# Nine places in place of six for split weight chunks, three of them in memory that the stages share, and another order of VectorE's work at the seams between stages

## The reference

```python
x = x + 0.5 * swiglu(rmsnorm(x), ...)              # f1, hidden size 2816
h = rmsnorm(x); a_in, q, k, v, g = split(h @ w_in)
y_a = spatial_gating(gelu(a_in), ...)              # group norms of one half, mixed over rows
y_b = stick_breaking_attention(q, k, v)            # 16 heads
x = x + (g_a * (y_a @ w_branch_a) + g_b * (y_b @ w_branch_b)) @ w_out
x = rmsnorm(x + 0.5 * swiglu(rmsnorm(x), ...))     # f2
x = layer_norm(ALPHA * x + gla_mixer(x))           # gated linear attention, 4 heads
x = layer_norm(ALPHA * x + swiglu_ffn(x))          # f3
x = layer_norm(ALPHA * x + moba_mixer(x))          # rotary, causal attention, 8 heads
x = layer_norm(ALPHA * x + swiglu_ffn(x))          # f4
```

## Time and profile before

| | |
|---|---|
| runs (3) | 1272.39, 1273.16, 1273.42 us; median 1273.16 |
| profiled execution | 1272.88 us, its span 1271.1 us |
| granted TensorE clock | 0.999 of full |
| PE busy | 1253.1 us (99% of the span) |
| DVE, ACT busy | 759.4 us (60%), 604.3 us (48%) |
| mean DMA rate | 178 GB/s |

### The profile page before, as it was taken

How to read it: one execution, slowest core, us unless ns; L and a number is a source line. 1 busy time by engine, 2 the same in 40 slices (tenths; PEclk the granted TensorE clock), 3 DMA queues, 4 the chain that set the end, 5 groups by cost and what they waited for, 6 DMA issues and landing times.

```text
span 1271.1 us, 15302 instructions
## 1 busy us (share of the span) xinstructions
PE 1253.1 (99%) x5989; PEld 1023.2 (80%) x5989; DVE 759.4 (60%) x1023; ACT 604.3 (48%) x780; POOL 43.7 (3%) x99
## 2 busy tenths in 40 slices
PE   8999999999999999999999999999999999999999
PEld 6888887887777888888877657888887887888887
DVE  5755556756676665555456557555557767655554
ACT  6444435556657454444345434444434554444441
POOL 2000002100000000000000010000000000000000
PEclk9999999999999999999999999999999999999999
DMA  7756554755445466555555336655564544755551
GB/s 264 216 182 199 184 181 158 251 179 144 145 154 188 152 199 208 187 195 185 168 155 169 106 128 199 214 189 184 189 198 152 197 139 127 241 188 167 193 186 52
DMA packets 119767, 226.03 MB, mean 178 GB/s; under 512 B 8056, under 2 KB 16256, under 8 KB 119696
## 3 DMA queue, kind: packets, MB, share of 16 engines
q1 hardware_dynamic: 117120, 216.10, 52.1%
q0 software_dynamic: 2560, 8.95, 2.6%
q10 hardware_dynamic: 16, 0.00, 0.0%
HBM read 223.98 MB, written 1.05 MB: 177 GB/s over the span
## 4 chain that ended last, share of the span: by engine, by line
PE 92%; DVE 5%; issue 1%; POOL 1%; ACT 1%; DMA 0%; DVEq 0%; POOLq 0%; ACTq 0%
PE ps L409 28%; PE ps L412 28%; PE ps L417 28%; PE ps L370 3%; DVE wl L1444 2%; DVE X L1534 1%; DVE X L1540 1%; PE ps L738 1%; PE ps L740 1%; PE ps L569 1%; PE ps L582 1%; PE ps L874 0%; DVE XTL L1482 0%; DVE st L1525 0%; DVE X L1545 0%
## 5 line engine op out<-in xcount | busy, mean ns | idle before, releaser
L1444 DVE TENSOR_TENSOR wl<-raw,wh 128x1024 fp32r<-128x1024 f32 x409 | 487.4, 1219 | 247.1 <-ACT wh L903 244.5
L903 ACT ACTIVATE wh<-raw 128x1024 fp32r<-128x1024 f32 x409 | 422.8, 1055 | 227.3 <-PE ps L417 199.3
L409 PE MATMUL ps<-wh,XTH 128*128 128x512 f32 (+1 forms) x1184 | 453.4, 386 | 1.9 <-ACT wh L903 1.9
L412 PE MATMUL ps<-wl,XTH 128*128 128x512 f32 (+1 forms) x1184 | 445.5, 380 | 4.7 <-DVE wl L1444 4.7
L417 PE MATMUL ps<-wh,XTL 128*128 128x512 f32 (+1 forms) x1184 | 347.0, 379 | 0.2 <-DVE XTL L1482 0.2
L409 PEld LDWEIGHTS ps<-wh,XTH 128*128 128x128 f32 x1184 | 223.1, 188 | 47.7 <-issue 4.7
L412 PEld LDWEIGHTS ps<-wl,XTH 128*128 128x128 f32 x1184 | 223.3, 189 | 47.4 <-DVE wl L1444 7.9
L417 PEld LDWEIGHTS ps<-wh,XTL 128*128 128x128 f32 x1184 | 215.9, 188 | 43.6 <-DVE XTL L1482 1.3
L409 PE MATMUL ps<-wh,HHf 128*128 128x512 f32 x352 | 137.8, 391 | 0.0
L412 PE MATMUL ps<-wl,HHf 128*128 128x512 f32 x352 | 137.1, 390 | 0.0
L417 PE MATMUL ps<-wh,HLf 128*128 128x512 f32 x352 | 108.4, 389 | 0.0
(11 more groups left out here) (279 smaller groups left out, 941.6 us busy)
## 6 DMA issues: line engine op xcount, KB each, us to landing
raw<-in_ffn_w_gu_dram SPq DMA_DIRECT2D x88, 512.0 KB, 4.5
raw<-in_w_in_dram SPq DMA_DIRECT2D x56, 512.0 KB, 3.7
raw<-in_ff_w_gate_dram SPq DMA_DIRECT2D x44, 512.0 KB, 4.5
raw<-in_ff_w_up_dram SPq DMA_DIRECT2D x44, 512.0 KB, 4.8
raw<-in_ff_w_down_dram SPq DMA_DIRECT2D x44, 512.0 KB, 4.1
raw<-in_ffn_w_down_dram SPq DMA_DIRECT2D x44, 512.0 KB, 4.4
raw<-in_gla_w_in_dram SPq DMA_DIRECT2D x24, 512.0 KB, 4.5
raw<-in_moba_w_in_dram SPq DMA_DIRECT2D x24, 512.0 KB, 4.6
```

The costliest lines, as they stand in the source:

```text
L409: e.matmul(o, lh[:, kt, rows(t)], wh[:, s, w], start=kt == 0, stop=False)
L412: e.matmul(o, lh[:, kt, rows(t)], wl[:, s, w], start=False, stop=False)
L903: e.activation(wh[:, j % NS, 0:m], raw[:, j % NR, 0:m], ACT.Copy).then_inc(S("wh"), 1)
L1444: e.tensor_tensor(wl[:, j % NS, 0:m], raw[:, j % NR, 0:m], wh[:, j % NS, 0:m].bitcast(F32), ALU.subtract).then_inc(S("wl"), 1)
```

## The change

The number of places becomes nine. The six private ones stay; three more, wh2 and wl2 (24 KB a partition), are the first tiles of the memory in which each stage lays out its own. In the feed-forward stages and the MoBA stage a placeholder tile keeps that memory free. In the mixer it holds Q, K and V from block q0 on, until the first chunk of wb1 has been used, and in the GLA stage VV, KE, QDT, KIT and part of SS from gv0 until the first chunk of go0 has been used; during these stretches (`held`) only six places are given out. Each chunk takes the place that was used longest ago. `reach(n)` is the last chunk that can be split when chunk n has been used: with nine places `reach(j - 2)` is j + 7, with six it is j + 4.

For the opening blocks VectorE is held to the block's own chunks ahead of the readout of t = 0, and ScalarE to the block's end plus one; in the closing blocks VectorE makes one call between the two readouts. The 24 spare products are taken out.

```diff
+            wh2, wl2 = [sb(n, [P, MORE, 1024], FR, phase) for n in ("wh2", "wl2")]
...
+            sb("more_f2", [P, 2 * MORE, 1024], F32, phase)
...
-            QG, KG, LA = [sb(n, [P, 2, 512], F32, phase) for n in ("QG", "KG", "LA")]
-            VV, GG, O = [sb(n, [P, 2, D], F32, phase) for n in ("VV", "GG", "O")]
-            KE = sb("KE", [P, 2, 512], F32, phase)
+            VV = sb("VV", [P, 2, D], F32, phase)
+            KE = sb("KE", [P, 2, 512], F32, phase)
+            QDT, KIT = [sb(n, [P, 4, 256], F32, phase) for n in ("QDT", "KIT")]
+            SS = sb("SS", [P, 2, 3, 256], F32, phase)
...
+        held = [(first_chunk("q0"), first_chunk("wb1")), (first_chunk("gv0"), first_chunk("go0"))]
+        place, freed = [], []
+        last_use = [-NS - MORE + i for i in range(NS + MORE)]
+        for j in range(len(chunks)):
+            for begin, end in held:
+                if j == begin:
+                    last_use[NS:] = [end] * MORE
+            i = min(range(NS + MORE), key=lambda i: (last_use[i], i))
+            place.append(i)
+            freed.append(last_use[i])
+            last_use[i] = j
...
+        def reach(n):
+
+            j = max(n + 1, 0)
+            while j < len(chunks) and freed[j] <= n:
+                j += 1
+            return j - 1
+
+        OPENING, CLOSING = ("f1g0", "vg0", "f2g0", "gq", "f3g0", "mq0", "f4g0"), ("f1d1", "wo1", "f2d1", "go1", "f3d1",
+                                                                                  "mo1", "f4d1")
...
-            spare(4, left, wh[:, 0, 0:512], [six, seven])
...
```

In `act_program`:

```diff
-                    if j >= NS:
-                        e.wait_ge(S("used"), j - NS + 1)
+                    if freed[j] >= 0:
+                        e.wait_ge(S("used"), freed[j] + 1)
...
-                high_to(at_chunk["step"] + LEAD)
+                high_to(reach(at_chunk["step"] - 1))
...
-                    high_to(j - 1 + LEAD)
+                    high_to(reach(j - 2))
...
-                    high_to(end - tail - 1 + LEAD)
+                    ahead = reach(end - tail - 2)
+                    high_to(min(ahead, end + 1) if name in OPENING else ahead)
                     yield 0
                     for j in range(end - tail, end - 2):
-                        high_to(j + LEAD)
+                        high_to(reach(j - 1))
```

In `dve_program`:

```diff
-                low_to(at_chunk["step"] + LEAD)
+                low_to(reach(at_chunk["step"] - 1))
...
-                    low_to(j - 1 + LEAD)
+                    low_to(reach(j - 2))
...
-                    low_to(end - tail - 1 + LEAD)
+                    ahead = reach(end - tail - 2)
+                    low_to(min(ahead, end - 1) if name in OPENING else ahead)
                     yield 0
-                    for j in range(end - tail, end - 2):
-                        low_to(j + LEAD)
+                    for j in range(end - tail, end - tail + 1 if name in CLOSING else end - 2):
+                        low_to(reach(j - 1))
```

More of the change, by code:

```diff
@@ L18 @@
 NS = 6
-LEAD = NS - 1
+MORE = 3
 NEG = -1e30
@@ L120, in build @@
         with ExitStack() as phase:
+            VV = sb("VV", [P, 2, D], F32, phase)
+            KE = sb("KE", [P, 2, 512], F32, phase)
+            QDT, KIT = [sb(n, [P, 4, 256], F32, phase) for n in ("QDT", "KIT")]
+            SS = sb("SS", [P, 2, 3, 256], F32, phase)
+            STm = sb("STm", [P, 2, 2, 64], F32, phase)
+            GG, O = [sb(n, [P, 2, D], F32, phase) for n in ("GG", "O")]
             QG, KG, LA = [sb(n, [P, 2, 512], F32, phase) for n in ("QG", "KG", "LA")]
-            VV, GG, O = [sb(n, [P, 2, D], F32, phase) for n in ("VV", "GG", "O")]
-            KE = sb("KE", [P, 2, 512], F32, phase)
             E1 = sb("E1", [P, 2, 512], F32, phase)
-            QDT, KIT = [sb(n, [P, 4, 256], F32, phase) for n in ("QDT", "KIT")]
-            STm = sb("STm", [P, 2, 2, 64], F32, phase)
-            SS = sb("SS", [P, 2, 3, 256], F32, phase)
             lowT = sb("lowT", [16, 256], F32, phase)
@@ L197, in build, with first_chunk, wh_of, wl_of @@
         plan_ffn("f4", ffn_w_gu[1, :, 0:FF], ffn_w_gu[1, :, FF:], ffn_w_down[1])
+        def first_chunk(name):
+            return blocks[name][1]
+        held = [(first_chunk("q0"), first_chunk("wb1")), (first_chunk("gv0"), first_chunk("go0"))]
[9 more added lines that the diff above has]
+            last_use[i] = j
+        def wh_of(j):
+            return wh[:, place[j], :] if place[j] < NS else wh2[:, place[j] - NS, :]
+        def wl_of(j):
+            return wl[:, place[j], :] if place[j] < NS else wl2[:, place[j] - NS, :]
+        def reach(n):
[5 more added lines that the diff above has]
+                                                                                  "mo1", "f4d1")
         ev_count, mm0_count, seen = {}, {}, [0] * 4
@@ L398, in pe_products @@
             b, at, end, width, kts = blocks[name]
-            s, (_, n, _, k0) = j % NS, chunks[j]
+            _, n, _, k0 = chunks[j]
+            high, low = wh_of(j), wl_of(j)
             o = ps[:, bank_of(name, t), 0:width]
@@ L408, in pe_products @@
                     wait(e, "h", t, kt)
-                e.matmul(o, lh[:, kt, rows(t)], wh[:, s, w], start=kt == 0, stop=False)
+                e.matmul(o, lh[:, kt, rows(t)], high[:, w], start=kt == 0, stop=False)
                 if t == 0 and c == 0:
                     e.wait_ge(S("wl"), j + 1)
-                e.matmul(o, lh[:, kt, rows(t)], wl[:, s, w], start=False, stop=False)
+                e.matmul(o, lh[:, kt, rows(t)], low[:, w], start=False, stop=False)
             for c in range(n):
@@ L416, in pe_products @@
                     wait(e, "l", t, kt)
-                ins = e.matmul(o, ll[:, kt, rows(t)], wh[:, s, w], start=False, stop=kt == kts - 1)
+                ins = e.matmul(o, ll[:, kt, rows(t)], high[:, w], start=False, stop=kt == kts - 1)
             if t == 1:
@@ L649, in pe_gla @@
             b, at, end, width, kts = blocks["low"]
-            o, s = ps[0:16, bank_of("low", 0), 0:256], at % NS
+            o = ps[0:16, bank_of("low", 0), 0:256]
             e.wait_ge(S(f"ev{bank_of('low', 0)}"), ev_count["low", 0] - 1)
@@ L653, in pe_gla @@
             for kt in range(8):
-                hw, lw = [w[:, s, kt * 16:kt * 16 + 16] for w in (wh, wl)]
+                hw, lw = [w[:, kt * 16:kt * 16 + 16] for w in (wh_of(at), wl_of(at))]
                 e.matmul(o, hw, XTH[:, kt, :], start=kt == 0, stop=False)
@@ L899, in high_to @@
                     m = chunks[j][1] * chunks[j][2]
-                    if j >= NS:
-                        e.wait_ge(S("used"), j - NS + 1)
+                    if freed[j] >= 0:
+                        e.wait_ge(S("used"), freed[j] + 1)
                     e.wait_ge(S(f"raw{j % NR}"), 16 * (j // NR + 1))
-                    e.activation(wh[:, j % NS, 0:m], raw[:, j % NR, 0:m], ACT.Copy).then_inc(S("wh"), 1)
+                    e.activation(wh_of(j)[:, 0:m], raw[:, j % NR, 0:m], ACT.Copy).then_inc(S("wh"), 1)
                     at_chunk["next"] += 1
             def more():
-                high_to(at_chunk["step"] + LEAD)
+                high_to(reach(at_chunk["step"] - 1))
             def block(name, tail=0):
@@ L1214, in gla @@
                         copy_first("gq", QG, cols(0))
-                high_to(blocks["low"][1] - 1 + LEAD)
+                high_to(reach(blocks["low"][1] - 2))
                 def split_o(half):
@@ L1443, in low_to @@
                     e.wait_ge(S("wh"), j + 1)
-                    e.tensor_tensor(wl[:, j % NS, 0:m], raw[:, j % NR, 0:m], wh[:, j % NS, 0:m].bitcast(F32),
+                    e.tensor_tensor(wl_of(j)[:, 0:m], raw[:, j % NR, 0:m], wh_of(j)[:, 0:m].bitcast(F32),
                                     ALU.subtract).then_inc(S("wl"), 1)
@@ L1901, in gla @@
                         copy_second("gq", QG, cols(0))
-                low_to(blocks["low"][1] - 1 + LEAD)
+                low_to(reach(blocks["low"][1] - 2))
                 e.wait_ge(S("used"), blocks["low"][2])
```

11 lines of the change are left out of this document (7 added, 4 removed).

## The result

| | before | after |
|---|---|---|
| median of the runs | 1272.78 us (4 runs, 1272.31 to 1273.42) | 1281.55 us (4 runs, 1279.92 to 1283.25) |
| ratio | | 1.0065, 95% interval 1.0053 to 1.0077 |
| profiled execution; its span | 1272.88; 1271.1 us | 1283.25; 1281.5 us |
| granted TensorE clock | 0.999 | 0.993 |

The mean clock of after also counts the last 3.7 us of the kernel, which are at half clock and in which TensorE has nothing to do; in before the 24 spare products stand there.

What follows compares the result with a forecast made beforehand. TensorE, busy 1253.1 of 1271.1 us, was taken as the bound, so only its waits could be won. Gains of 7.4 and losses of 10.2 us gave +2.8 on 1272.88: 1275.7 us, range 1270 to 1279.3.

Steps and rivals of the forecast that it cites:

- Part 1: Stage openings: the last rows of a layer norm start earlier, a gain of 7.4 us together.
- Part 2: Places where three more splits come ahead of something TensorE needs: a loss of 10.2 us together.
- spare products: Kernel end: taking out the 24 products beside the last norm changes nothing, bounds 0 and 0.2 us.
- f1: Feed-forward f1 at the start: nine splits instead of seven make HB late, a loss of 1.9 us.
- wo0: wb1 and wo0: three more splits ahead of the merge delay YAL, a loss of 1.4 us, bounds 0.6 and 1.7.
- gk: GLA opening: QG's copy behind the split of gv0's late first chunk, a loss of 3.8 us, bounds 0 and 4.6.
- vg1: Mixer opening: first vg1 chunk split behind the group norm, 3.3 us lost, 1.4 us wait gone, net loss 1.9.
- MoBA key block: Between MoBA opening and key readout: rotary product late for the head transposes, 1.2 us loss, bounds 0 and 1.8.
- Rival 4: All upper bounds: U as late as now, wo0, GLA, MoBA at upper ends, late go0 load: 1279.2 us, chance 0.15.
- Rival 1: Parameter loads do not hold the weights up; losses of 3.8 and 1.2 us go: 1270.7 us, chance 0.17.
- rival 2: Catch-up hidden everywhere but in the mixer, readouts not behind the new splits: 1267.4 us, chance 0.1.
- rival 3: No effect: five raw buffers, not places, set the lead; seams and catch-ups both shrink: 1272.9 within 1, chance 0.08.

Runs made afterwards that it cites:

- settled version: Changed kernel with catch-ups held back at f1, wb1 to wo0 and gq to gk, and vg1's first chunks split before the group norm: 1263.98 us, ratio 0.9925.
- vg1 run: Changed kernel, but VectorE splits the first chunk of vg1 ahead of the group norms of vg0: 1278.40 us, ratio 1.0039 to before.
- GLA run: Changed kernel, but only six places are given out from gq to gk: 1274.94 us, ratio 1.0009 to before.

## Why the prediction was right or wrong

**Part 1 was right.** Every opening gained what was worked out for it: f3 and f4 1.7 and 1.6 (1.6), MoBA 2.0 (2.0), GLA 1.3 (1.0), f2 and mixer 0.7 each (0.6). The steps behind it, one split between the readouts and XTL ahead of the splits, stand in the timelines. The runs with nine places and the old order, and with the closing order alone, show that the closing half needs the opening half; whether the opening half needs the other was not run.

**Part 2 had four of the five places right, and one step wrong at all four of them.** The step that failed is that a wait of TensorE was priced at its own length alone; the granted clock was looked at only for the spare products at the end. In the kernel before, no wait behind the first 12 us is longer than 1.3 us by its record, and the clock is full from there to the last product, so nothing in that part prices a longer one. There was a sign: its one earlier stretch at half clock, from 8.52 to 11.93, comes just behind waits of 1.3 and 0.8 us. The prediction passed over it. The runs put a price on it: one stretch of 3.41 us at half clock, 1.7 us, and with four of them 6.8 of the 7.6 us by which the sum was short in the profiled executions. Adding 6.8 to the forecast gives 1282.5; the median is 1281.55 (how many stretches the other three runs had is not recorded). That the clock fell because TensorE idled is shown by the run that kept it busy.

What is left are sizes. Their sum is only 0.8 us, but that is partly luck: f1, wo0 and gk were too small by 1.8, 0.5 and 1.1, while vg1, the MoBA key block and the gains make up for 2.5 of it.
- f1: 3.2 us of idling for 1.9. The term counted the splits rightly (nine for seven) but not that GpSimd's wait for the fifth low half moves with it. The late start is in the traces, and TensorE doesn't wait for HB in the settled version, where the hold is off, while it waits 1.0 us where six places and the hold stand together.
- vg1: 2.7 us of idling, 2.9 with the bracket's 0.2, for 3.3. U came 1.2 to 1.9 us earlier, for 1.5.
- wo0: the wait was ScalarE's for its raw chunk, which the text had only as a possible wait. 1.7 for 1.4.
- gk: 4.8, 5.0 with the bracket's 0.2, for 3.8. The prediction has the late chunk on its way from 652.3 to 662.3, 10.0 us; it took 11.0, from 662.81 to 673.78, and that is most of the difference.
- MoBA key block: 0 for 1.2. VectorE was in time: five splits run back to back and MK is copied at 1002.67, which is the time of the earlier trace rows shifted by TensorE's own 12.1 us. Two splits, 2.3 us, fitted into the 2.54 idle; that the chunk would land late was not so. Bound 0 held. VectorE's timeline of after:

```profile
996.93 5.76 DVE L1473 TENSOR_TENSOR wl<-raw,wh 128x1024 fp32r<-128x1024 f32 x5
1002.67 0.69 DVE L2059 COPY MK<-ps 128x512 f32<-128x512 f32 x1
```

- Spare products: 0, held.
- Slips that move nothing: the sum has the MoBA key block at 1.2 and the list of what the profile should show has 1.4; the terms of vg1 and gk come to 3.2 and 3.9 by their own figures, not 3.3 and 3.8.

**Rivals.** Rival 4 (all upper bounds, 1279.2) came nearest by luck: it had no clock, and of its conditions U as late as now and the MoBA upper end did not come. Rival 1 and rival 2 fell with the waits at gk and HB, rival 3 with the gains at the seams. The direction came out as the likeliest of the three, the range did not hold the time: its bounds took in the unknown lengths of waits, and not what follows a wait.

## What to carry to other kernels

In a kernel that keeps TensorE at 99% with waits under 1.5 us, a new wait of 2 us or more is priced at its length plus the stretch at half clock behind it, 1.7 us here and 3.4 where the stretch was twice as long. A deeper buffer has a cost where the lead grows: the catch-up stands in every list ahead of the next readout, so let it grow by one split at a time and behind the readouts that somebody waits for. When an item is moved back in one engine's list, search the other lists for constants that count it (`wait_ge(S("wl"), 5)`).

## What the runs showed of the hardware

- Behind the first 14 us and ahead of the kernel's end, every stretch at half clock in the twelve traces goes with a wait of TensorE: it begins between 2.3 us ahead of the wait's end and 1.5 us behind it. It lasts 3.41 us, or 6.83 (at gk in the vg1 run, at vg1 in the GLA run, and four times in the run with six places and the new order). Idling of 2.1 us and more (waits for QG, HB, wl, XTL and YAH) always had one; waits of 1.4 us and less none; at 1.7 to 1.8 us, the wait for YAH, it went either way: half clock behind 1.7 us in after, none behind 1.8 us in the run with gq held. At the start of the kernel it is otherwise: in before one stretch follows waits of 1.3 and 0.8 us. Runs of one version scatter with such stretches, as far as can be argued from one trace each: eleven runs of the version with gq held went from 1271.62 us (clock 0.997) to 1276.63 (0.994).
- Products that nobody reads, put into a wait, kept the clock full: 53 of them made the kernel 4.9 us faster.
- The weight chunk that goes out 2 us behind the load of the GLA norm gain (repeated rows of 1 KB) landed after 11.0 us, against 4.5 in the median of the weight chunks in the earlier trace rows. It was no different in before, where the seven weight chunks that go out from 651.7 to 667.5 took 10.2 us in the median and 12.9 at most. The gain itself took 9.7 us again (part 6 of the page of after), where other loads of the same size by GpSimd took 3.8 to 6.0. That the repeated rows are the cause, as the prediction has it, is not shown: two smaller loads go out right behind the gain, of 32 and 256 KB, and they took 9.1 and 10.4 us. In this time the DMA engines are busy but move little, 87 GB/s, and 383 GB/s in the window behind it (view by windows and view of issues of after):

```profile
663.00:670.00 7.00, 7.00 (x42) 5.65 (x41) 4.41 (x4) 2.92 (x4) 0.00 (x0) 1.00 0.89 87
671.00:677.00 6.00, 1.23 (x6) 0.73 (x5) 2.05 (x3) 2.11 (x2) 0.00 (x0) 1.00 1.01 383
```

```profile
gbc<-in_gla_norm_g_dram POOLq DMA_DIRECT2D x1, 512.0 KB, 9.7
bgk<-in_gla_b_gk_dram POOLq DMA_DIRECT2D x1, 256.0 KB, 10.4
wgk<-in_gla_w_gk_dram POOLq DMA_DIRECT2D x1, 32.0 KB, 9.1
gbc<-in_final_norm_dram POOLq DMA_DIRECT2D x1, 512.0 KB, 3.8
```
